# A fused two-block transformer kernel: the first block's step order changed, and the recurrent branch kept in PSUM

## The reference

```python
# first block
h = rmsnorm(x, attn_norm_g)
gla_q, gla_k, gla_v, gla_r, gla_lr, mb_q, mb_k, mb_v, mem_q = split(h @ w_in)
g_log = log_sigmoid(gla_lr @ w_gla_gk + b_gla_gk) / 16
o_gla = rmsnorm(gla_chunked(gla_q, gla_k, gla_v, g_log), gla_out_norm_g) * silu(gla_r)
o_moba = moba_attention(rmsnorm(mb_q), rmsnorm(mb_k), mb_v)        # 4 heads of 64
mem_k, mem_v = split(rmsnorm(mem, mem_norm_g) @ w_mem_kv)          # 256 memory tokens
o_mem = memory_attention(rmsnorm(mem_q), rmsnorm(mem_k), mem_v)
x = x + concat(o_gla, o_moba, o_mem) @ w_out
x = x + hierarchical_moe(rmsnorm(x), ...)                          # 32 experts, top 2
# second block
u_x, u_g, q, k, v, g_lru, g_att = split(rmsnorm(x) @ w_in_2)
c = causal_depthwise_conv(u_x, conv_w, conv_b)                     # 4 taps
r, i = sigmoid(c @ w_rgate + b_r), sigmoid(c @ w_igate + b_i)      # 16 diagonal blocks of 64
log_a = -8 * r * softplus(-lam)
u = sqrt(-expm1(2 * log_a)) * (i * c)
y_lru = scan(h = exp(log_a) * h + u) * gelu(u_g)                   # over the 512 tokens
merged = sigmoid(g_lru) * (y_lru @ w_br_lru) + sigmoid(g_att) * (stick_breaking(q, k, v) @ w_br_att)
x = x + merged @ w_out; x = x + relu(h2 @ w_up)**2 @ w_down; x = x + sigmoid(h3 @ w_ple_gate) * (p @ w_ple)
out = rmsnorm(x)
```

## Time and profile before

| | |
|---|---|
| median of 3 runs | 1845.45 us (1844.28 to 1849.76) |
| the profiled execution, its own time | 1845.85 us |
| its span, first to last instruction | 1843.4 us |
| PE busy | 1723.0 us, 93% |
| DVE, ACT, POOL busy | 702.5, 603.2, 563.2 us |
| TensorE clock granted, mean | 0.973 |

### The profile page before, as it was taken

One profiled execution on the slowest core, in us unless ns is written; L12 is line 12 of the kernel. 1 busy time (PEld: TensorE's weight loads), 2 busy tenths in 40 slices (PEclk: granted clock), 3 DMA queues, 4 the chain that ended last, 5 costly groups with the idle time before them and its releaser, 6 DMA issues.

```text
span 1843.4 us, 20373 instructions
## 1 busy us (share of the span) xinstructions
PE 1723.0 (93%) x8350; PEld 1202.3 (65%) x8350; DVE 702.5 (38%) x1058; ACT 603.2 (33%) x786; POOL 563.2 (31%) x263
## 2 busy tenths in 40 slices
PE   8789888799999999988789999999999999999995
PEld 5577655444444443445578987777778788888882
DVE  5544543333433333357851012223344421222335
ACT  5545444111001110124631245554333432322231
POOL 2232224321022201013244434443443444444440
PEclk9889989899999999999999999999999999999997
DMA  5121163499999999961222110111242222222201
GB/s 202 46 69 47 46 248 132 176 419 421 422 421 421 421 421 420 421 254 62 76 91 92 46 47 27 66 46 48 94 178 91 92 92 92 92 92 97 87 35 46
DMA packets 75069, 308.57 MB, mean 167 GB/s; under 512 B 3008, under 2 KB 4448, under 8 KB 50272
## 3 DMA queue, kind: packets, MB, share of 16 engines
q1 hardware_dynamic: 74704, 306.18, 42.5%
q0 software_dynamic: 272, 1.05, 0.2%
HBM read 305.12 MB, written 2.10 MB: 167 GB/s over the span
## 4 chain that ended last, share of the span: by engine, by line
PE 82%; DVE 10%; ACT 4%; issue 2%; POOL 1%; DMA 0%; DVEq 0%; SPq 0%; ACTq 0%
PE ps L846 39%; PE ps L1178 12%; PE ps L888 7%; PE ps L1202 6%; PE ps L1132 4%; PE ps L844 2%; PE ps L1325 2%; PE ps L1147 1%; PE ps L1148 1%; PE ps L1310 1%; ACT sb_slot L1392 1%; PE ps L1346 1%; DVE sb_R L2304 1%; POOL sb_w_parts L786 1%; DVE sb_slot L1797 1%
## 5 line engine op out<-in xcount | busy, mean ns | idle before, releaser
L786 POOL TENSOR_TENSOR sb_w_parts<-sb_slot,sb_w_parts 128x2048 fp32r<-128x2048 f32 x59 | 274.5, 4654 | 411.3 <-ACT sb_w_parts L1392 411.3
L846 PE MATMUL ps<-sb_h_high,sb_w_parts 128*128 128x512 f32 x1120 | 273.3, 396 | 15.5 <-issue 8.2
L846 PEld LDWEIGHTS ps<-sb_h_high,sb_w_parts 128*128 128x128 f32 x1120 | 210.9, 189 | 67.3 <-issue 12.7
L1178 PE MATMUL ps<-sb_slot,sb_hT 128*64 128x512 f32 x768 | 171.1, 594 | 0.0
L1392 ACT ACTIVATE sb_w_parts<-sb_slot 128x2048 fp32r<-128x2048 f32 x59 | 112.7, 1911 | 172.4 <-PE ps L846 172.4
L846 PE MATMUL ps<-sb_hidden_high,sb_w_parts 128*128 128x512 f32 x704 | 165.2, 389 | 1.8 <-ACT sb_hidden_high L1392 1.8
L846 PEld LDWEIGHTS ps<-sb_hidden_high,sb_w_parts 128*128 128x128 f32 x704 | 132.1, 188 | 29.7 <-ACT sb_hidden_high L1392 2.3
L750 POOL TENSOR_TENSOR sb_tile_parts<-sb_slot,sb_tile_parts 128x1024 fp32r<-128x1024 f32 x32 | 76.3, 2387 | 221.5 <-ACT sb_tile_parts L1392 221.5
L846 PE MATMUL ps<-sb_h_low,sb_w_parts 128*128 128x512 f32 x560 | 138.0, 389 | 0.0
L1178 PEld LDWEIGHTS ps<-sb_slot,sb_hT 128*64 128x64 f32 x768 | 53.6, 137 | 106.2 <-issue 106.2
L846 PEld LDWEIGHTS ps<-sb_h_low,sb_w_parts 128*128 128x128 f32 x560 | 105.1, 188 | 21.8
(11 more groups left out here) (312 smaller groups left out, 2675.2 us busy)
## 6 DMA issues: line engine op xcount, KB each, us to landing
sb_slot<-w_up SPq DMA_DIRECT2D x24, 2048.0 KB, 15.5
sb_slot<-w_gate SPq DMA_DIRECT2D x24, 2048.0 KB, 15.4
sb_slot<-w_down SPq DMA_DIRECT2D x21, 2048.0 KB, 16.2
sb_slot<-w_in SPq DMA_DIRECT2D x14, 2048.0 KB, 8.0
sb_R<-w_down SPq DMA_DIRECT2D x11, 2048.0 KB, 15.8
sb_slot<-tiles SPq DMA_DIRECT2D x32, 512.0 KB, 3.4
sb_R<-w_gate SPq DMA_DIRECT2D x8, 2048.0 KB, 15.2
sb_R<-w_up SPq DMA_DIRECT2D x8, 2048.0 KB, 15.8
```

The source lines that it names most:

```text
L786: nc.gpsimd.tensor_tensor(low, raw_part(g), high.bitcast(F32), ALU.subtract).then_inc(w_low, 1)
L846: ins = nc.tensor.matmul(o, w[:, k, at:at + P], h[:, k, :], start=first, stop=last)
L1178: ins = nc.tensor.matmul(ps_[b * CAP:(b + 1) * CAP, bank0, :], xgT[:, k, at:at + CAP], w[:, b, kk * 512:(kk + 1) * 512], start=(k == 0), s ...
```

## The change

In the first block: the weight conversions (`w1`) that belong to a pair's fills are emitted ahead of that pair's softmax step; memory's squares and sums come earlier; the row norms of gla are split in two steps and spread over pairs 11 and 12; `intra 1` moves from behind pair 12 to ahead of it; `lam` moves from pair 12 to pair 14; `silu` and `mix` of heads 0 and 1 move ahead of the last `gla_out`. In the second block: `norm_sum` follows the third ux tile and no longer the second; a ux tile is normed within its PSUM bank, and the taps read the bank; the gates of a pair are asked for one pair of tiles later; the input gate's sigmoid stays in its bank; the square of the decay is a third exponential on ACT; the gelu works within the bank, and its product (`gated_out`) comes one tile later.

```diff
+
+    def split_to(g):
+
+        while split[0] <= min(g, len(TILES1) - 1):
+            step("w1", split[0])
+            split[0] += 1
+
     def tile(name, n):
 
-        g = TILES1.index((name, n))
-        if g + 1 < len(TILES1):
-            step("w1", g + 1)
+        split_to(TILES1.index((name, n)) + 1)
         job("tile", name, n)
 
...
              ["gla_out", 1]]
-    middle = {2: ["mem_sum"]}
-    late = {0: ["mem_parts"], 1: ["mem_acc"], 2: [("decay", 0)], 4: [("decay", 1)], 5: [("decay_qk", 0)], 8: [("turn_keys", 0), ("intra", 0)],
-            9: [("chunk_state", 0)], 10: [("decay_qk", 1)], 11: [("gla_sum", 0), ("turn_keys", 1)], 12: [("intra", 1), "lam"],
-            13: [("chunk_state", 1)]}
+    late = {0: ["mem_acc"], 1: ["mem_sum"], 2: [("decay", 0)], 4: [("decay", 1)], 5: [("decay_qk", 0)], 8: [("turn_keys", 0), ("intra", 0)],
+            9: [("chunk_state", 0)], 10: [("decay_qk", 1)], 11: [("gla_sum", 0), ("turn_keys", 1), ("intra", 1), ("gla_norm", 0, 0)],
+            12: [("gla_norm", 0, 1)], 13: [("chunk_state", 1)], 14: ["lam"]}
 
     def gla(kind, *arg):
...
-    step("w1", 0)
+    split_to(0)
     step("x_parts")
-    step("w1", 1)
-    job("tile", "mk", 0)
+    tile("mk", 0)
     step("x_squares")
     tile("mq", 0)
+    step("mem_parts")
     step("norm", 0)
     step("evict", "mk", 0)
     step("evict", "mq", 0)
     tile("mv", 0)
     step("evict", "mv", 0)
     job("lr")
+    step("mem_low")
     post("mk", 0)
...
+            if fills[i][0] != "gla_out":
+                split_to(TILES1.index(fills[i][0]) + 1)
             step("soft", i)
         if i >= 2:
             step("low", i - 2)
         if i < len(PAIRS):
             step("norm_rows", i)
-            if i == 2:
-                step("mem_recip")
+            if i == 15:
+                step("silu", 0, 2)
+                step("mix", 0)
+                step("mix", 1)
             if fills[i][0] == "gla_out":
                 gla(*fills[i])
             else:
@@ -156,14 +164,14 @@
                 gla(*((e,) if type(e) is str else e))
         elif i == len(PAIRS):
             gla("gla_sum", 1)
-            step("silu", 0, 2)
+            step("gla_norm", 1, 0)
             tile("r", 2)
             step("evict", "r", 2)
-            step("mix", 0)
-            step("mix", 1)
+            step("gla_norm", 1, 1)
     tile("r", 3)
     step("silu", 2, 3)
     step("mix", 2)
+    split_to(TILES1.index(("out", 1)))
...
             if base in ("ux", "ug"):
-                pair = n // 2 - 1 + (4 if base == "ug" else 0)
-                if 0 <= pair < 4:
-                    if n % 2 == 0:
-                        for m in (2 * pair, 2 * pair + 1):
-                            job("lru_gate", "r", m)
-                            job("lru_gate", "i", m)
-                    elif base == "ug":
-                        step("lru", pair)
-                if base == "ux" and n % 2:
-                    step("conv", n // 2)
-                    if pair >= 0:
-                        step("lru", pair)
+                j = n + (KD if base == "ug" else 0)
+                if j % 2 and 5 <= j <= 11:
+                    step("lru_in", (j - 5) // 2)
+                    step("lru", (j - 5) // 2)
+                if j % 2 == 0 and 4 <= j <= 10:
+                    for m in (j - 4, j - 3):
+                        job("lru_gate", "r", m)
+                        job("lru_gate", "i", m)
             if base == "out2":
                 step("feed", 4, n)
...
                     taken(act, ("lru_gate", "r", 2 * g + 1))
                     for m in (2 * g, 2 * g + 1):
                         fn(la[:, m % 2, :], lr_[:, m % 2, :], ACT.Exp, scale=nsp8[:, m:m + 1])
-                        ins = fn(lt[:, m % 2, :], lr_[:, m % 2, :], ACT.Tanh, scale=sp8[:, m:m + 1])
+                        link(fn(lt[:, m % 2, :], lr_[:, m % 2, :], ACT.Tanh, scale=sp8[:, m:m + 1]))
+                        ins = fn(lr_[:, m % 2, :], lr_[:, m % 2, :], ACT.Exp, scale=nsp16[:, m:m + 1])
                     ins.then_inc(lru_exp, 1)
+                elif kind == "lru":
+                    g = arg[0]
                     act.wait_ge(lru_m2, g + 1)
                     fn(lt, lt, ACT.Sqrt).then_inc(lru_mult, 1)
                 elif kind == "stick":
...
-                        dve.wait_ge(pad_zero, 1)
-                        normed(uxp[:, n % 2, 3:3 + S], st)
+                        o, c_ = bank(st), lc[:, n, :]
+                        finished(dve, st)
+                        dve.wait_ge(high_done, KD)
+                        link(v.tensor_tensor(o, o, rstd, ALU.mult))
+                        link(v.tensor_scalar(c_, o, G("conv_w_2", 24 + n), G("conv_b_2", n), ALU.mult, ALU.add))
+                        for tap in (2, 1, 0):
+                            late = 3 - tap
+                            ins = v.scalar_tensor_tensor(out=c_[:, late:S], in0=o[:, 0:S - late], scalar=G("conv_w_2", 8 * tap + n),
+                                                         in1=c_[:, late:S], op0=ALU.mult, op1=ALU.add)
+                            if tap:
+                                link(ins)
+                        frees(ins, st)
                     elif name == "q2":
                         finished(dve, st)
...
-                        dve.wait_ge(ug_done, n + 1)
-                        v.tensor_tensor(yl[:, n, :], yl[:, n, :], gel[:, n % 2, :], ALU.mult).then_inc(yl_done, 1)
+                        finished(dve, st)
+                        v.tensor_tensor(bank(st), bank(st), rstd, ALU.mult).then_inc(ug_in, 1)
+                        if n:
+                            gated_out(n - 1)
+                        if n == KD - 1:
+                            gated_out(n)
                     elif name in ("bl", "ba"):
                         sg_ = sig["gl" if name == "bl" else "ga"][:, n, :]
...
 
                     overflow(dve, n_over, over)
-                elif kind == "conv":
+                elif kind == "lru_in":
                     g = arg[0]
                     for m in (2 * g, 2 * g + 1):
+                        dve.wait_ge(in_gate, m + 1)
                         taken(dve, ("proj", "ux", m))
-                        dve.wait_ge(pad_zero, 1)
-                        c_, u_ = lc[:, m % 4, :], uxp[:, m % 2, :]
-                        link(v.tensor_scalar(c_, u_[:, 3:3 + S], G("conv_w_2", 24 + m), G("conv_b_2", m), ALU.mult, ALU.add))
-                        for tap in (2, 1, 0):
-                            ins = v.scalar_tensor_tensor(out=c_, in0=u_[:, tap:tap + S], scalar=G("conv_w_2", 8 * tap + m), in1=c_,
-                                                         op0=ALU.mult, op1=ALU.add)
-                            if tap:
-                                link(ins)
-                        ins.then_inc(conv_done, 1)
+                        frees(v.tensor_tensor(li[:, m % 2, :], bank(("lru_gate", "i", m)), lc[:, m, :], ALU.mult), ("lru_gate", "i", m))
+                    dve.wait_ge(lru_exp, g + 1)
+                    v.scalar_tensor_tensor(out=lt, in0=lr_, scalar=1.0, in1=lt, op0=ALU.add, op1=ALU.mult).then_inc(lru_m2, 1)
                 elif kind == "lru":
                     g = arg[0]
-                    dve.wait_ge(lru_exp, g + 1)
-                    taken(dve, ("lru_gate", "i", 2 * g))
-                    taken(dve, ("lru_gate", "i", 2 * g + 1))
-                    dve.wait_ge(conv_done, 2 * g + 2)
-
-                    link(v.tensor_tensor(lr_, la, la, ALU.mult))
-                    v.scalar_tensor_tensor(out=lt, in0=lr_, scalar=1.0, in1=lt, op0=ALU.add, op1=ALU.mult).then_inc(lru_m2, 1)
-                    link(v.tensor_tensor(li, li, lc[:, 2 * g % 4:2 * g % 4 + 2, :], ALU.mult))
+                    for m in (2 * g, 2 * g + 1):
+                        taken(dve, ("lru_gate", "i", m))
                     dve.wait_ge(lru_mult, g + 1)
                     link(v.tensor_tensor(lt, lt, li, ALU.mult))
                     for m in (2 * g, 2 * g + 1):
```

76 lines of the change are left out of this document (40 added, 36 removed).

## The result

| | before | after |
|---|---|---|
| median | 1847.04 us (1844.28 to 1851.29, 5 runs) | 1833.96 us (1832.66 to 1836.0, 5 runs) |
| profiled execution, its span | 1845.85, 1843.4 us | 1833.53, 1831.4 us |
| TensorE clock granted, mean | 0.973 | 0.974 |

The ratio is 0.9935, 95% interval 0.9921 to 0.9949: some 12 us faster, less than half of the 26.5 forecast.

A forecast was written before the change was run, and what follows sets the result against it. TensorE, 93% busy, was taken as the bound, so time was a sum of shifts: 3.9 + 7.7 + 5.9 − 2.6 + 11.9 less 0.3 gives 26.5 us, recurrence 0; 1845.85 − 26.5 = 1819.3, said as 1819, range 1803 to 1836.

The forecast's parts named there:

- Start and memory's sums: First block's start: 0.3 us lost at the first root, 3.9 us gained as cq0 starts behind pair 0's values.
- 0, at worst −2: First root, behind memory's copies and square on ACT: ready 0.4 us before TensorE wants it, so 0, at worst −2 us.
- no term above would change: The claim that the DVE and GpSimd exclusion rule, hitting scans but not the new taps, alters none of the forecast's sizes.
- cv0: Tile cv0, first block: weights converted early, so gq0 starts 9.7 us sooner, less 1.9 for POOL and later transpositions: 7.7 us gained.
- cv1: Tile cv1, first block: no wait for converted weights, by the same working as cv0 6.4 − 0.5 = 5.9 us gained.
- Rival (B): First block gives back half, as removed waits covered others in the softmax chain: 13.5 us gained, 1832 us; chance 0.20.
- Pairs 11 to 16: First block: 5.3 us gained at intra 1, 7.9 lost to lam, silu and mixes with a little slow clock: −2.6 us.
- Out tiles: End of first block: four waits of 7.52 us and about 4.5 us of slow matmuls go: 11.9 us gained.
- Recurrence: Second block's recurrent branch: DVE's loop no shorter, later start made up, new waits before ug4 and ug6: 0, range −6 to +10.
- rival (A): Both parts pay: POOL's subtraction falls beside PSUM taps, not scans, 15 us more gained, 1804 us; chance 0.17.
- Experts and tail: Expert stage and everything after the recurrent branch: shifts whole with what comes before, 0 us change.
- one with a single SBUF input goes free: The skill's rule as quoted: such a DVE instruction isn't blocked by GpSimd, so the new taps are immune.

The follow-up runs named there:

- Kernels 3 and 4: Changed kernel with memory's low part later on DVE; the second also with ACT's memory copies and squares behind the first root: both 1833.8 us, ratios to before 0.9937, 0.9938.
- Kernel 13: Changed kernel with cv1's weight copy alone left behind pair 5's exponentials, as before the change: 1837.43 us, ratio to before 0.9941.
- kernel 10: Changed kernel with lam moved from pair 14 to the fourth last out tile: 1828.66 us, ratio to before 0.9914.
- kernel 9: Changed kernel with the recurrence's panel weights copied ahead of each pair's exponentials, not behind its root: 1820.99 us, ratio to before 0.9874.
- kernel 12: Changed kernel plus kernel 9, kernel 10, earlier norm_sum, gated_out ahead of scans, memory's copies behind the root, its low part behind its sums: 1812.95 us, ratio to before 0.9827.
- kernel 14: First block changed, recurrent branch as before the change but with panel weights copied ahead of each pair's exponentials: 1832.52 us, ratio to before 0.9928.
- kernels 5 and 13: The first: changed kernel with gla's three DVE products (decay_qk 0) moved from behind pair 5 to behind pair 6, 1839.16 us, ratio to before 0.9957. The second: see Kernel 13.
- kernel 1: First block in its new order, recurrent branch as before the change: 1833.13 us, ratio to before 0.9932.

## Why the prediction was wrong

The direction and most steps held; the sum did not: 26.5 us were forecast, 12 came. Two of its terms are also added up wrongly by a little: 9.7 − 1.9 is 7.8 and not 7.7, and the four slow groups named for the out tiles, each against half, give 3.9 us and not 4.5.

- **Start and memory's sums** (−0.3, +3.9): −4.2 and +4.4. Of the −4.2, 0.65 stood already at mk1 and lies within the scatter there. The failed step is the one on the root, "0, at worst −2": it walked ACT and left out that `mem_low` puts eight DVE instructions with two SBUF inputs beside POOL's subtraction for mk1. The rule of the Trainium skill that I quoted covers just this, in the other direction from the scans; "no term above would change" was wrong. Kernels 3 and 4 show the cause, 2.0 us and with the slow clock 3.6; no kernel kept a gain from moving that work.
- **cv0** (+7.7): +7.9, with the 2 us that POOL and DVE cost each other as foreseen. Right.
- **cv1** (+5.9): gv0 led by 4.9 more, and 4.2 of it were gone at gv1. The failed step is taking a tile's wait as gain without walking the softmax chain to the next `turn`; it is the largest miss. Kernel 13 shows that 5 of 7 us were cover. Rival (B) named this mechanism, and its time, 1832, is within 2 us of the median, in part by luck: it gave 13 us to this mechanism in the whole block and none to the recurrence, where the runs show it at cv1 alone for certain.
- **Pairs 11 to 16** (−2.6): −4.3, as r0's gain was 3.8 and not 5.3: the wait of 4.06 us and the slow clock behind it went, but gv1 began at a slower clock (4.52 us for 4.00), and three short waits of 0.61, 0.53 and 0.26 us are new. The cost of `lam` and the mixes, −7.9, was right to 0.2 us in its sum, but not in its parts: `lam` was over half of it (kernel 10), where the forecast gave it 2.2.
- **Out tiles** (+11.9): +10.7 from r2 on, 1.5 of slow clock in r2 among it; all four waits gone. Right.
- **Recurrence** (0, −6 to +10): −3.4, inside its own range but not 0. The mechanism held: roots came at most 2 us later than placed, and the new waits before ug4 and ug6 stood some 2 us behind where they were expected. Mis-sized was the end of ug7, placed at 951.8 us in the old count and measured at 955.1, a miss of 3.3 us: 2 of it are the late start of ug6, the rest arises behind that. The forecast's reason against rival (A), that the copy is queued behind the root, is what kernel 9 removed: it was worth 13 to 15 us in the stage, near (A)'s 15.
- **Experts and tail** (0): −1.4 and +1.7. In the last pair of experts 16 matmuls took 5.35 us and not 3.65, behind the same wait of 0.8 us as in the kernel before.

In the first block 26.5 became 15.1: 3.4 went at the start and memory's sums together, 5.2 in and behind cv1, 1.5 in pairs 11 and 12, 1.2 in the out tiles.

## What to carry to other kernels

A wait on the bounding engine is worth its length only up to the next chain that was hidden behind it: after each removed wait, walk the other engines to their next hand-over before the gain is booked, and measure it some tiles behind the place, since the 3 us that kernel 12 won at cq0 were gone at gq0. Then look at what a copy triggers. A copy on one engine that releases a long two-input operation on another should be queued where the third engine reads PSUM or stands still, and not behind the step that ends in scans from SBUF.

## What the runs showed of the hardware

- **DVE and POOL exclude each other both ways.** Two subtractions 7.02 us and eight low parts 5.33 us together, 4.80 and 3.24 apart; scans up to 5.55 us beside POOL and 1.21 without; taps with one PSUM input 0.746 to 0.752 us in kernel 9 with POOL beside them, those with two SBUF inputs up to 5.16 in kernel 14. The Trainium skill's "SBUF — State Buffer", section "Who interferes with whom", states both sides, and these rows agree. It excepts the two-port modes of instructions like the first tap, which the prediction's "one with a single SBUF input goes free" left out: beside POOL a first tap from SBUF took 2.85 us (2.83 in kernel 14) and not 0.54.
- **The first tap costs more from PSUM**, 0.81 us against 0.54 from SBUF:

```profile
L2284 DVE TENSOR_SCALAR sb_R<-sb_R,sb_prm x8: 537/541/2851, 838.8 to 895.5; 128x512 f32<-128x512 f32 x8
```

  The Trainium skill's "VectorE: DVE Perf Modes", section "Why PSUM operands drop a tier", says that a PSUM operand bars the faster mode for float32; the row agrees in direction, at 1.5 times.
- **The clock after one and the same wait is not the same.** Behind a wait of 1.2 us TensorE went on at 2.4 GHz in one kernel and ran at 1.2 GHz for some 10 us in two others, kernels 5 and 13 (0.71 against 1.22 us for the same four matmuls), and the executions of kernel 1 fell in two groups, 0.978 at 1828 and 0.972 to 0.974 at 1833 to 1836. What decides was not settled; it puts some 5 us on any single profile of this kernel.
- **A table load took 1.28 us** in all sixteen profiles, with the next function right behind it (in kernel 9 a load at 871.19 and the root at 872.49).
